# Sparse weight tiles joined and attention steps moved in a two-block network's first projection

## The reference

```python
gq, gk, gv, gg, mq, mk, mv, mo, mg = _split(h @ w_in, EVEN_SIZES)
log_a = [(jax.nn.log_sigmoid(((h @ a1[d]) @ a2[d] + ab[d]).astype(jnp.float32)) / GLA_TAU)
         .reshape(bsz, t, GLA_HEADS, GLA_DK) for d in range(2)]
qk = jax.nn.silu(dwconv1d(jnp.concatenate([mq, mk], axis=-1), conv_w, conv_b))
gates = (mg + gate_b).astype(jnp.float32).reshape(bsz, t, 4, ML_HEADS)
...
    rel = jnp.where(tri, cum[:, :, None] - cum[:, None, :], -jnp.inf)
    att = jnp.einsum('bthk,bshk,btshk->bhts', qc, kc, jnp.exp(rel))
    o = jnp.einsum('bhts,bshv->bthv', att, vc) + jnp.einsum('bthk,bhkv->bthv', qc * jnp.exp(cum), s)
```

## Time and profile before

| What | us |
|---|---|
| Median of 3 runs | 1794.82 |
| Lowest, highest | 1794.4, 1798.31 |
| The profiled execution's own time | 1799.98 |
| Its span in the trace | 1798.3 |
| TensorE busy (94%) | 1698.9 |
| VectorE busy (75%) | 1345.1 |
| ScalarE busy (47%) | 847.9 |

### The profile page before, as it was taken

One profiled execution on the slowest core, in us unless ns is written; L12 is line 12 of the kernel. 1 busy time (PEld: TensorE's weight loads), 2 busy tenths in 40 slices (PEclk: granted clock), 3 DMA queues, 4 the chain that ended last, 5 costly groups with the idle time before them and its releaser, 6 DMA issues. The chain is left out here.

```text
span 1798.3 us, 26476 instructions
## 1 busy us (share of the span) xinstructions
PE 1698.9 (94%) x10222; PEld 1448.4 (81%) x10222; DVE 1345.1 (75%) x2521; ACT 847.9 (47%) x1476; POOL 55.4 (3%) x113
## 2 busy tenths in 40 slices
PE   4899999898999999999999998999998999999997
PEld 3788877676888888877788766988897988989997
DVE  6678884876999999968984678699965555765594
ACT  2623335635544443245553565333344467665541
POOL 0910000000000000000000000000000000000000
PEclk9999999999999999999999999999999999999998
DMA  8343441031222226733553333554555454344452
GB/s 318 119 152 125 127 132 51 29 112 70 94 94 94 94 94 220 236 129 129 174 167 119 117 100 113 182 158 152 153 188 178 147 172 151 129 127 134 140 166 81
DMA packets 70150, 245.90 MB, mean 137 GB/s; under 512 B 7951, under 2 KB 9480, under 8 KB 69768
## 3 DMA queue, kind: packets, MB, share of 16 engines
q1 hardware_dynamic: 68024, 241.52, 41.5%
q10 hardware_dynamic: 2000, 2.69, 0.5%
HBM read 242.80 MB, written 1.11 MB: 136 GB/s over the span
## 5 line engine op out<-in xcount | busy, mean ns | idle before, releaser
L462 PE MATMUL banks<-m,weights_high 128*128 128x256 f32 (+1 forms) x4336 | 1045.0, 334 | 31.3 <-DVE weights_low L498 24.7
L462 PEld LDWEIGHTS banks<-m,weights_high 128*128 128x128 f32 x4336 | 737.2, 192 | 124.9 <-issue 23.3
L462 PE MATMUL banks<-m,weights_low 128*128 128x256 f32 (+1 forms) x2168 | 716.8, 331 | 0.0
L498 DVE TENSOR_TENSOR weights_low<-weight_ring,weights_high 128x1024 fp32r<-128x1024 f32 x293 | 355.5, 1222 | 226.8 <-ACT weights_high L493 225.9
L462 PEld LDWEIGHTS banks<-m,weights_low 128*128 128x128 f32 x2168 | 415.4, 192 | 37.5
L493 ACT ACTIVATE weights_high<-weight_ring 128x1024 fp32r<-128x1024 f32 x293 | 309.0, 1057 | 233.2 <-PE banks L462 152.9
L630 DVE SCALAR_TENSOR_TENSOR m<-m,columns 128x189 f32<-128x189 f32 (+4 forms) x856 | 321.8, 450 | 24.9 <-ACT m L570 24.7
L769 DVE SCALAR_TENSOR_TENSOR m<-weight_ring,m 128x1024 bf16<-128x1024 f32 x184 | 225.1, 1223 | 18.0 <-DMA weight_ring<-in_weights 12.2
L569 ACT ACTIVATE m<-banks,columns 128x512 f32<-128x512 f32 (+1 forms) x120 | 83.2, 693 | 303.8 <-PE banks L462 303.7
L462 PE MATMUL banks<-m,weight_ring 128*128 128x256 f32 x704 | 152.1, 379 | 0.0
L462 PEld LDWEIGHTS banks<-m,weight_ring 128*128 128x128 f32 x704 | 133.7, 190 | 18.1
(11 more groups left out here) (395 smaller groups left out, 1580.2 us busy)
## 6 DMA issues: line engine op xcount, KB each, us to landing
weight_ring<-in_weights SPq DMA_DIRECT2D x433, 512.0 KB, 3.7
m<-entering SPq DMA_DIRECT2D x32, 256.0 KB, 3.3
x<-in_tokens SPq DMA_DIRECT2D x1, 2048.0 KB, 14.3
m<-in_cmp_w SPq DMA_DIRECT2D x1, 2048.0 KB, 7.4
m<-in_cond SPq DMA_DIRECT2D x2, 512.0 KB, 4.9
out<-x ACTq DMA_DIRECT2D x8, 128.0 KB, 1.9
columns<-in_columns SPq DMA_DIRECT2D x1, 633.0 KB
m<-in_rg_w ACTq DMA_DIRECT2D x1, 512.0 KB, 3.5
```

Of the source, the lines that this page charges most:

```text
L462: mm = pe.matmul(out, lhsT, rhs, start=p.start and i == 0, stop=p.stop and i == len(passes) - 1)
L498: dve.tensor_tensor(w_lo[:, g % PARTS, :], K.ring[:, PLACE[PRODUCT_BLOCKS[g]] % RING, :], w_hi[:, g % PARTS, :].bitcast(F32), ALU.subtract ...
```

## The change

First, the weight tiles of `low`, `li` and `lf` become one. The item's bank is then emptied three times: rows of `low` (53, with the added one for the bias `ab`), `li` (36) and, from partition 64, `lf` (36, a plain copy; its bias is added later by one activation in `MlstmGates.logarithms`). Items 9 and 10 are gone, there are 29 items, and `even_in` has 29 blocks; `mq` and `mk` are items 9 to 16. Second, the distances of level 1 stand at tick 10, ahead of the scores of the diagonal (still 11); its factors at 12, its scores at 13. Third, the other levels' distances stand at 14, 18, ... 34 (before 17, 21, ... 37), their factors one tick later, their scores three ticks later; the sums at 38 (before 41). The steps behind the sums have ticks less by four, which is the two items. The two `gg` pairs wait for their own half of the keys. On VectorE the log decays have a yield of their own behind the read of the decays.

```diff
-    ("mod0", 48 * KD), ("mod1", 48 * KD), ("even_in", 31 * KD), ("even_out", 8 * 8), ("up0", 2 * KF * KD),
+    ("mod0", 48 * KD), ("mod1", 48 * KD), ("even_in", 29 * KD), ("even_out", 8 * 8), ("up0", 2 * KF * KD),
...
-    one(biased(f["low"], 49, "low_one"))
+    def first_rows(act, bank):
+        for name, m in (("low", LOW_ROWS), ("li", MlstmGates.R)):
+            act.activation(f[name][0:m, :], bank[0:m, :], ACT.Identity, bias=K.col("first_b", rows=slice(0, m)), scale=1.0)
+        return act.activation(f["lf"][0:MlstmGates.R, :], bank[64:64 + MlstmGates.R, :], ACT.Copy)
+
+    one(first_rows)
...
-    one(biased(f["li"], 36, "ml_li_b"))
-    one(biased(f["lf"], 36, "ml_lf_b"))
...
-    DECAYS, DIAGONAL, LEVELS, SPACING = 6, 11, 13, 4
-    SUMS, KEYS, STATES, OUTPUTS, END = 41, (44, 46), (48, 50, 52), (54, 56), 61
+    DECAYS, DIAGONAL = 6, 11
+    LEVELS, FACTORS, SCORES = ((first, *range(second, 38, 4)) for first, second in ((10, 14), (12, 15), (13, 17)))
+    SUMS, KEYS, STATES, OUTPUTS, END = 38, (40, 42), (44, 46, 48), (50, 52), 57
...
-        yield self.DIAGONAL
-        pe.wait_ge(*self.emptied(4))
-        pe.wait_ge(*self.absed.at(1))
-        pe.wait_ge(*self.z_read.at(1))
-        scores(f["gq"], f["gk"])
         for l in range(1, GLEVELS + 1):
-            yield self.level(l)
-            pe.wait_ge(*self.taken.at(l))
+            at, _, scores_at = self.level(l)
+            yield at
+            if l == 1:
+                pe.wait_ge(*self.absed.at(1))
+                pe.wait_ge(*self.la_made.at(1))
+            else:
+                pe.wait_ge(*self.taken.at(l))
             pe.wait_ge(*self.tabled.at(l))
-            pe.wait_ge(*self.la_made.at(1))
             distances(self.between[:, 2 * l - 2, :], self.between[:, 2 * l - 1, :])
-            yield self.level(l) + 3
+            if l == 1:
+                yield self.DIAGONAL
+                pe.wait_ge(*self.emptied(4))
+                pe.wait_ge(*self.exps.at(1))
+                scores(f["gq"], f["gk"])
+            yield scores_at
+            if l == 1:
+                pe.wait_ge(*self.taken.at(1))
             pe.wait_ge(*self.made.at(l))
...
+        yield self.DECAYS + 2
         dve.wait_ge(*self.logged.at(1))
...
+        link(act.activation(self.lf, self.lf, ACT.Identity, bias=self.K.col("ml_lf_b", rows=slice(0, self.R)), scale=1.0))
         link(act.activation(e, self.lf, ACT.Abs))
```

More of the change, by code:

```diff
@@ L1156, in _ @@
             sync.dma_start(K.cols[:], K.dram["columns"]).then_inc(*loads.up(16))
-            sync.dma_start(a2[0:49, :], K.dram["gla_a2"]).then_inc(*loads.up(16))
+            sync.dma_start(a2[0:LOW_ROWS, :], K.dram["gla_a2"]).then_inc(*loads.up(16))
             load_weights(K, sync, 0)
@@ L1284, in put @@
         return empty
-    def biased(dest, m, bias):
-        return lambda act, bank: act.activation(dest[0:m, :], bank[0:m, :], ACT.Identity,
-                                                bias=K.col(bias, rows=slice(0, m)), scale=1.0)
     def tokens(empty):
@@ L1318, in even_projection @@
     for j in range(4):
-        one(put(f["gg"][:, j, :], ACT.Copy, after=gla.keys_ended))
+        one(put(f["gg"][:, j, :], ACT.Copy, after=lambda j=j: gla.keys_ended(j)))
     tokens(lambda i: put(f["mo"][:, i, :], ACT.Sigmoid, after=gla.outputs_made))
@@ L1377, in all_scored, with keys_ended @@
         return self.scored.at(GLEVELS + 1)
-    def keys_ended(self):
-        return self.keyed.at(2)
+    def keys_ended(self, row):
+        return self.keyed.at(1 + row // 2)
     def outputs_made(self):
@@ L1554, in scalar_steps @@
         for l in range(1, GLEVELS + 2):
-            yield self.SUMS if l > GLEVELS else self.level(l)
+            yield self.SUMS if l > GLEVELS else self.level(l)[0]
             act.wait_ge(*self.dists.at(l))
@@ L1618, in vector_steps @@
         for l in range(1, GLEVELS + 1):
-            yield self.level(l) + 1
+            _, factors_at, scores_at = self.level(l)
+            yield factors_at
             size, half = 1 << l, 1 << (l - 1)
@@ L3439, in lay_out @@
     gq, gk, gv, gg, mq, mk, mv, mo, mg = np.split(w, np.cumsum([256, 256, 512, 512, 512, 512, 512, 512]), axis=1)
-    small = np.zeros((D, 3, P), f32)
-    small[:, 0, 0:16], small[:, 0, 32:48] = v["gla_a1"][0, 0], v["gla_a1"][0, 1]
-    small[:, 1, 0:4], small[:, 1, 32:36] = mg[:, 0:4], mg[:, 8:12]
-    small[:, 2, 0:4], small[:, 2, 32:36] = mg[:, 4:8], mg[:, 12:16]
-    parts["even_in"] = [feature_tiles(small[:, 0]), feature_tiles(gq), feature_tiles(gk), token_tiles(gv),
-                        feature_tiles(small[:, 1]), feature_tiles(small[:, 2]), feature_tiles(mq), feature_tiles(mk),
-                        token_tiles(mv), feature_tiles(gg), token_tiles(mo)]
+    small = np.zeros((D, P), f32)
+    for d in range(2):
+        small[:, 32 * d:32 * d + MH] = mg[:, 8 * d:8 * d + 4]
+        small[:, 32 * d + LOW_AT:32 * d + LOW_ONE] = v["gla_a1"][0, d]
+        small[:, 64 + 32 * d:64 + 32 * d + MH] = mg[:, 8 * d + 4:8 * d + 8]
+    parts["even_in"] = [feature_tiles(small), feature_tiles(gq), feature_tiles(gk), token_tiles(gv), feature_tiles(mq),
+                        feature_tiles(mk), token_tiles(mv), feature_tiles(gg), token_tiles(mo)]
     parts["even_out"] = [feature_tiles(v["even_w_out"][0])]
-    a2 = np.zeros((49, 256), f32)
-    a2[0:16], a2[32:48] = v["gla_a2"][0, 0], v["gla_a2"][0, 1]
-    a2[16], a2[48] = v["gla_ab"][0, 0], v["gla_ab"][0, 1]
+    a2 = np.zeros((LOW_ROWS, 256), f32)
+    for d in range(2):
+        a2[32 * d + LOW_AT:32 * d + LOW_ONE], a2[32 * d + LOW_ONE] = v["gla_a2"][0, d], v["gla_ab"][0, d]
     w = v["ssd_w_in"][0]
@@ L3496, in lay_out @@
     gb = v["ml_gate_b"][0]
-    for name, a in (("ml_li_b", 0), ("ml_lf_b", 4)):
-        cols[0:4, COL[name]], cols[32:36, COL[name]] = gb[a:a + 4], gb[8 + a:12 + a]
+    for d in range(2):
+        cols[32 * d + LOW_ONE, COL["first_b"]] = 1.0
+        cols[32 * d:32 * d + 4, COL["first_b"]], cols[32 * d:32 * d + 4, COL["ml_lf_b"]] = gb[8 * d:8 * d + 4], gb[8 * d + 4:8 * d + 8]
     put("ssd_conv_w", taps(v["ssd_conv_w"][0]))
```

13 lines of the change are left out of this document (7 added, 6 removed).

## The result

The changed kernel takes 1805.37 us (median of 6 runs, 1803.57 to 1808.7); the kernel before, run beside it, 1797.95 (1794.4 to 1800.55, 6 runs). The ratio is 1.0046, with a 95% interval of 1.0034 to 1.0058: 8.3 us slower by the ratio (6.1 to 10.4). The direction was forecast. Of the 5.0 us between 1800.4 and 1805.37, 3.1 are the kernel before itself, whose median was 1794.82 in the three runs known then; the other 1.8 are the change, 7.4 by the medians and sized at +5.6.

A forecast was written before the change was run, and what follows sets the result against it. TensorE, busy 94%, was taken to bound the kernel. Terms -10.9 + 1.1 + 2.9 + 5.5 + 5.4 - 0.7 = +3.3, plus 2.3 for the clock, made +5.6 on 1794.82: 1800.4 us, range 1790.5 to 1805.

The forecast's parts named there:

- Part 1: Joined weight tiles: 48 matmuls of 512 columns go where TensorE has no gap, -10.9 us.
- Part 2: First item: three ScalarE emptyings instead of one delay block 3's split and all behind it, +1.1 us.
- That wait stays as it is: The value tiles' 3.6 us wait for item 4's emptying was to stay unchanged, as the whole 1.1 us shift goes through.
- Part 3: Level 1 ahead of the diagonal: TensorE waits at level 1's scores for the last factor product, +2.9 us.
- Part 4: Takes now behind VectorE's convolution: distances of levels 4 to 6 wait 1.8 us each (+5.5), level 7's +5.4.
- Rival A: Faster: the convolution does not hold the takes back, distances of levels 4 to 7 don't wait; 1787 to 1790 us, chance 0.12.
- Rival B: No change: one or two of the forecast waits are not there; 1792 to 1797 us, chance 0.13.
- rival C: Slower still: block 15's doubled modulation pair or a late weight load costs at most 2.4 us each; 1803 to 1807, chance 0.07.
- The sums' 0.7: TensorE's wait at the sums goes, as level 7's take no longer has a split ahead of it, -0.7 us.
- +3.3: Sum in us of all forecast matmul and wait terms, with the granted clock as it is.
- the clock term: TensorE at its lower clock behind three long new waits: 0 to 5.1 us, taken as 2.3.
- The last sums pair: Sign in VectorE's timeline: begins near 288.6 us, up to 1.7 later per new stretch at 0.50; near 278 if Rival A holds.

The follow-up runs named there:

- Experiment 2: Changed kernel with level 1's factor products one half tile earlier (tick 11), directly behind the diagonal's take on VectorE: 1801.83 us, ratio 1.0024.
- experiments 1 and 3: Changed kernel with takes of levels 3 to 6 put ahead of the convolution: 1794.12 us; with levels 3 to 7 and sums on other half tiles: 1795.75 us.
- rows_53: Kernel before with four unused rows added to the small table loaded ahead of the first weights (53 instead of 49): 1799.12 us, ratio 1.0008.
- experiment 5: Joined weight tiles as in the changed kernel, but attention steps in the order and spacing of the kernel before: 1800.46 us, ratio 1.0023.
- both_filled_b: Changed kernel with takes ahead of the convolution, level 1's factors at 11, and 22 constant matmuls in TensorE's wait at 73 us: 1788.77 us, ratio 0.9956.

## Why the forecast had the direction and not the size

- **Part 1, -10.9: right.** 48 matmuls less; the stage's busy time without what the stretches at 0.50 cost is 10.3 less.
- **Part 2, +1.1: right for its first half.** The wait grew from 1.65 to 2.80. "That wait stays as it is" (L1283) held in two profiles of three; in the third 0.97 came back.
- **Part 3, +2.9: right.** From the diagonal's scores to S1 are 10.49 us (101.36 to 111.85) against a foreseen 10.4. Experiment 2 took the wait out and gained 3.5.
- **Part 4, +5.5 and +5.4: right in cause and order, a little high.** The waits are 1.53 three times and 5.07. Between the starts D4 to D6 are 1.7 late each and D7 5.2 (203.54 to 213.62, less 4.84); experiments 1 and 3 show the cause from two sides. Rival A is dead: nothing overtook on VectorE. Rival B's missing waits were all there, rival C's 2.4 us at block 15 were not.
- **The sums' 0.7 went, as foreseen.** The waits were forecast at +14.2 in all and measured +12.6, so with the clock as it is +3.3 becomes +1.7.
- **The failed step is the clock term**, "I take a little under half, 2.3". It measured 5.5 to 6.1, above its own bound of 5.1. The bound counted three new waits with one stretch of 3.41 each, and nothing at the waits that were there before. In fact the stage has four stretches more than before (17.07 against 3.41 us): of the twelve waits of 2.6 us and more in the three profiles of after five brought a double stretch, five a single one and two none, and the old wait near 90 brings a double one where the one at 73 brings none. Each costs half its length, 1.7, so four are up to 6.8; only 0.9 to 2.6 of the 17.07 us lay within a wait. What the prediction said of waste within a wait was thus no ground to halve the term.
- The Trainium skill's rule for this term ("TensorE: Matmul & The Clock Gate", Part 1) would have left it out. For the comparison that does not hold: the term is most of the difference. Nor do the traces bear out its ground, under 1% of the span, for this whole kernel: the three profiles of after have 61.2 to 75.2 us at 0.50 in spans of 1801.6 to 1805.8, so up to 1.7 to 2.1% is lost, less where TensorE waited anyway. What the skill prices is the ramp at a start; the stretches here lie mostly behind waits.
- **A term that was not there**: the table of 53 rows, which the sum leaves out, puts the first modulation back by some 1.5 us and the stage's start by 1.6 (means of three profiles). Every profile with 53 rows shows it; the timed runs of rows_53 bound it between -1.4 and +4.3.
- **The last sums pair** begins at 294.13, 294.40 and 295.90 us. Forecast were 288.6 plus 1.7 for each new stretch: with four stretches 295.4. That fits partly by luck: the mark leaves out the start's 1.6, and the waits came out 1.6 shorter than forecast.
- **The base** was the median of three runs, 1.5 to 3.2 us below that of later runs of the same kernel (1796.3 to 1798.0). It is 3.1 of the 5.0 us by which the time missed 1800.4.
- **In sum**, by the profiles: 5.6 forecast, +3.2 to 3.8 by the clock, +1.6 by the start, -1.6 by the waits, and up to 0.6 by the matmuls, make 9.4.

Open are what decides between no, one and two stretches behind a wait of 2.6 us and more, and whether the kernel before would have had none in more profiles.

## What to carry to other kernels

When work is taken out ahead of a hand-set order, ask for each step not only how far it moves but in which half of an item it lands, and what stands between the halves on the engine that must answer: here one half tile of parity cost 11 us, and two lines won it back. A gain in matmuls was worth nothing while the steps beside them kept their places (experiment 5). A wait of TensorE of 2.6 to 5.1 us cost more than its length: 46 of them in the 18 profiles of this stage brought 51 stretches of 3.41 us (none at 8, one at 25, two at 13), an estimated 1.9 us each on average. Check in the traces how a small table ahead of the weights is moved, and compare stages over several profiles before believing a difference of a few us.

## What the runs showed of the hardware

- The lower clock level did not follow from the length of one wait alone: 2.77 us brought 0, 3.41 or 6.83 us at 0.50 in nearly equal kernels (one or two stretches in 8 of 9 profiles), 1.53 none in 24 cases, 5.07 always one or two stretches (8 of 8 profiles). The sum in the stage was yet the same, 17.07 us, in five profiles.
- The number of rows of one small transfer (1 KB a row) ahead of the weights moved VectorE's first modulation: 10.04 to 10.18 us with 49 rows, 10.80 with 64, 11.33 to 11.84 with 53. Its packets took 0.42 to 0.57, 1.45 and 2.25 us; the 53 started one behind the other, 0.042 us apart.
- A matmul of f32 constants (L424, 128 columns) took 0.22 us (22 in 4.83 us, both_filled_b) and stands in a timeline as two.
